# Starting a kernel's mixing projection inside the last attention pair

## The reference, cut to what matters

```python
def mla_group(...):                       # 8 heads of 64
    q = rms_norm(q, g_qnorm); k = rms_norm(k, g_knorm)      # then rope on 32 of 96 columns
    pr = softmax(mask(q @ k.T * scale)); o = pr @ v
    o = rms_norm(o, g_attn_out)           # per head
def rwkv7_group(...):                     # 8 heads of 64
    ...                                   # y: layer norm per head, * ln_x_w + ln_x_b, + bonus
    return y * g
h = h + concat([mla, rwkv]) @ w_o_2       # 1024 x 1024: the "mix" stage
h = h + peer_ffn(rms_norm(h), ...)        # the next stage
```

## Time and profile before

| | us |
|---|---|
| median of three runs | 2223.5 |
| the profiled execution | 2227.96 |
| its span in the trace | 2226.2 |
| TensorE busy, of the span | 2168.6 (97%) |
| VectorE busy | 1467.3 (66%) |
| ScalarE busy | 1021.1 (46%) |
| mean granted TensorE clock | 0.991 |

### The profile page before, as it was taken

How to read it: one execution, slowest core, us unless ns; L and a number is a source line. 1 busy time by engine, 2 the same in 40 slices (tenths; PEclk the granted TensorE clock), 3 DMA queues, 4 the chain that set the end, 5 groups by cost and what they waited for, 6 DMA issues and landing times.

```text
span 2226.2 us, 42388 instructions
## 1 busy us (share of the span) xinstructions
PE 2168.6 (97%) x15414; PEld 1945.2 (87%) x15428; DVE 1467.3 (66%) x2785; ACT 1021.1 (46%) x1734; POOL 59.3 (3%) x59
## 2 busy tenths in 40 slices
PE   9999999999999999999998889999999999999999
PEld 7999998899899977999987558889888999999998
DVE  5556997655655556655765556989886666666665
ACT  4345775434534346443641343338634444444443
POOL 0000000000010000000000000110000000000000
PEclk9999999999999999999999989999999999999999
DMA  6555654455476534555511023434576666665664
GB/s 216 190 179 180 214 175 147 158 187 182 164 235 193 198 107 140 177 180 189 180 58 32 19 94 128 144 129 158 182 248 215 225 207 206 206 183 188 187 185 136
DMA packets 107727, 374.14 MB, mean 168 GB/s; under 512 B 11985, under 2 KB 17889, under 8 KB 107377
## 3 DMA queue, kind: packets, MB, share of 16 engines
q1 hardware_dynamic: 102848, 354.88, 48.6%
q0 software_dynamic: 4784, 18.00, 2.8%
HBM read 362.29 MB, written 13.69 MB: 169 GB/s over the span
## 4 chain that ended last, share of the span: by engine, by line
PE 92%; DVE 5%; ACT 1%; DVEq 1%; issue 1%; DMA 0%; ACTq 0%; POOL 0%
PE bank L351 70%; PE bank L380 8%; PE bank L1613 3%; PE bank L2513 3%; DVE w_lo L303 1%; PE bank L600 1%; PE bank L333 0%; ACT w_hi L298 0%; PE bank L618 0%; PE bank L335 0%; PE bank L2129 0%; PE bank L340 0%; DVE arena L1985 0%; PE bank L2465 0%; PE bank L2153 0%
## 5 line engine op out<-in xcount | busy, mean ns | idle before, releaser
L303 DVE TENSOR_TENSOR w_lo<-ring,w_hi 128x1024 fp32r<-128x1024 f32 x576 | 696.7, 1223 | 407.8 <-ACT w_hi L298 405.5
L298 ACT ACTIVATE w_hi<-ring 128x1024 fp32r<-128x1024 f32 x581 | 605.8, 1057 | 617.3 <-PE bank L351 561.5
L351 PE MATMUL bank<-u_hi,w_hi 128*128 128x256 f32 x2568 | 728.5, 284 | 1.9 <-DVE w_lo L303 1.9
L351 PE MATMUL bank<-u_hi,w_lo 128*128 128x256 f32 x2568 | 726.7, 283 | 0.0
L351 PE MATMUL bank<-u_lo,w_hi 128*128 128x256 f32 x2568 | 726.6, 283 | 0.0
L351 PEld LDWEIGHTS bank<-u_hi,w_hi 128*128 128x128 f32 x2568 | 492.2, 192 | 12.5 <-DVE w_lo L303 4.0
L351 PEld LDWEIGHTS bank<-u_lo,w_hi 128*128 128x128 f32 x2568 | 492.2, 192 | 7.4 <-issue 0.5
L351 PEld LDWEIGHTS bank<-u_hi,w_lo 128*128 128x128 f32 x2568 | 492.2, 192 | 0.0
L351 PE MATMUL bank<-w_hi,x_hi 128*128 128x512 f32 x992 | 391.5, 395 | 2.7 <-DVE x_lo L2719 1.3
L351 PE MATMUL bank<-w_lo,x_hi 128*128 128x512 f32 x992 | 389.3, 392 | 0.0
L351 PE MATMUL bank<-w_hi,x_lo 128*128 128x512 f32 x992 | 386.8, 390 | 0.0
(11 more groups left out here) (312 smaller groups left out, 1782.5 us busy)
## 6 DMA issues: line engine op xcount, KB each, us to landing
ring<-in_w SPq DMA_DIRECT2D x264, 512.0 KB, 3.7
ring<-in_expert_u SPq DMA_DIRECT2D x128, 512.0 KB, 3.5
ring<-in_expert_v SPq DMA_DIRECT2D x128, 512.0 KB, 4.2
ring<-in_ssm_in SPq DMA_DIRECT2D x40, 512.0 KB, 4.5
gate_dram<-con SPq DMA_DIRECT2D x16, 576.0 KB, 2.8
arena<-gate_dram POOLq DMA_DIRECT2D x9, 1024.0 KB, 8.6
ring<-in_ssm_out SPq DMA_DIRECT2D x16, 512.0 KB, 4.1
ring<-in_w_o SPq DMA_DIRECT2D x16, 512.0 KB, 3.6
```

Of the source, the lines that this page charges most:

```text
L298: act.activation(w_hi[slot][:, :], ring[slot][:, :], ACT.Copy).then_inc(hi_made[slot], 1)
L303: dve.tensor_tensor(w_lo[slot][:, :], ring[slot][:, :], w_hi[slot][:, :].bitcast(F32), ALU.subtract).then_inc(freed[slot], 1)
L351: mm = pe.matmul(out, left[a], right[b], start=start and n == 0, stop=stop and n == 2, skip_group_check=True)
```

## The change

Three things are altered; nothing that is computed changes.

- The mix stage's eight closings are taken in the order of tiles 4, 5, 6, 7, 0, 1, 2, 3 (recurrent tiles first), in slots 2, 3, 0, 1, 2, 3, 0, 1, and written out without loops. TensorE clears the accumulators and runs closings 0 and 1 between the scores and the probabilities of pair 3, closing 2 between probabilities and outputs, closing 3 between the outputs and `output_squares(3)`. Closings 4 to 7 follow behind it. The last two keep their order by quarters. ScalarE's and VectorE's splits for closings 0 to 5 are placed in the mla stage by hand.
- SyncE loads the first two weight tiles between the second and the third load of the mla heads, the other six behind the fourth.
- The seven passes on `y_rw` go into two of VectorE's waits for the rotation: L2299, L2302 and L2313 into `turn_head(1, 0)`, L2315 into `turn_head(2, 0)`.

```diff
+        MIX_OUT = ((2, 0), (3, 0), (0, 0), (1, 0), (2, 1), (3, 1), (0, 1), (1, 1))
+        MIX_TILE = (4, 5, 6, 7, 0, 1, 2, 3)
+        def mix_close(pe, p, quarters=range(4)):
+            n, i = MIX_OUT[p]
+            pe.wait_ge(S("left_ready"), left_no("mix_out", 0, p) + 1)
+            close_split(pe, p % 2, n, "mix_out", i, p == 7, quarters)
+        def mix_left_hi(act, p):
+            if p > 1:
+                m, j = MIX_OUT[p - 2]
+                split_done(act, m, "mix_out", j)
+            if p < 4:
+                act.wait_ge(S("m_max"), 5)
+            else:
+                act.wait_ge(S("mo_ready"), MIX_TILE[p] + 1)
+            act.activation(x_hi[:, p % 2, :], mix_all[:, MIX_TILE[p], :], ACT.Copy).then_inc(S("left_hi"), 1)
@@ mla_sync
             for i in range(4):
                 load(sp, i % 2, io["mla_u"][i, :, :], "mla_heads", i // 2)
+                if i == 1:
+                    mix_load(sp, 0)
+                    mix_load(sp, 1)
+            for p in range(2, 8):
+                mix_load(sp, p)
@@ mla_tensor
                     head_keys(pe, i + 1, 1)
+                else:
+                    pe.wait_ge(S("mo_ready"), 3)
+                    clear_acc(pe, upd["mix"])
+                    mix_close(pe, 0)
+                    mix_close(pe, 1)
                 turn_probs(i)
                 if more:
                     head_squares(pe, i + 1, 1)
                     turn_halves(i + 1, 0)
+                else:
+                    mix_close(pe, 2)
                 outputs(i)
+            mix_close(pe, 3)
             output_squares(3)
@@ mla_scalar
                     square_head(act, i + 1, 1)
+                else:
+                    mix_hi(act, 3)
+                    mix_left_hi(act, 2)
+                    mix_left_hi(act, 3)
                 for a in range(2):
                     act.wait_ge(S("mp_turned"), 2 * i + a + 1)
...
                     root_head(act, i + 1, 1)
+                else:
+                    mix_hi(act, 4)
+                    mix_left_hi(act, 4)
                 act.wait_ge(S("mo_done"), i + 1)
                 act.activation(mo_sq, group(i)[3][:, 0:T], ACT.Square).then_inc(S("mo_squared"), 1)
+                if i < 2:
+                    mix_hi(act, i)
+                elif i == 2:
+                    mix_left_hi(act, 0)
+                    mix_left_hi(act, 1)
+                else:
+                    mix_hi(act, 5)
+                    mix_left_hi(act, 5)
                 act.wait_ge(S("mo_summed"), i + 1)
                 rstd(act, mo_root, group(i)[2][:, 0:T], HD, stat[:, 14:15]).then_inc(S("mo_rooted"), 1)
+                if i == 2:
+                    mix_hi(act, 2)
@@ mla_vector, turn_head: between L2288 and L2290
+                if (i, a) == (1, 0):
+                    scale_recurrent()
+                if (i, a) == (2, 0):
+                    gate_recurrent()
+                if (i, a) == (3, 0):
+                    mix_lo(dve, 0)
@@ mla_vector, the loop
             for i in range(4):
                 for a in range(2):
+                    if i == 3:
+                        if a == 1:
+                            mix_lo(dve, 1)
+                        mix_left_lo(dve, a)
                     dve.wait_ge(S("m_scores"), 2 * i + a + 1)
...
                         turn_head(i + 1, a)
+                else:
+                    for p in range(2, 6):
+                        mix_lo(dve, p)
+                        mix_left_lo(dve, p)
                 dve.wait_ge(S("mo_rooted"), i + 1)
@@ the mix stage
         def mix_tensor(pe):
-            pe.wait_ge(S("mo_ready"), 4)
-            out_tensor(pe, "mix_out", upd["mix"])
+            mix_close(pe, 4)
+            mix_close(pe, 5)
+            for quarters in (range(3), (3,)):
+                mix_close(pe, 6, quarters)
+                mix_close(pe, 7, quarters)
```

More of the change, by code:

```diff
@@ L397, in clear_acc @@
                           skip_group_check=True)
[L402 to L405, removed]
         def left_no(stage, i, n):
@@ L410, in left_no @@
             return sum(4 * RING_PLAN[r][0] for r in order[:order.index(stage)]) + 4 * i + n
[L412 to L450, removed]
         ATTN_OUT = ((2, 0), (3, 0), (0, 0), (1, 0), (2, 1), (0, 1), (1, 1), (3, 1))
@@ L2111, in mla_sync, with mix_load, mix_hi, mix_lo @@
                 load(sp, i % 2, io["mla_u"][i, :, :], "mla_heads", i // 2)
+                if i == 1:
[5 more added lines that the diff above has]
+        MIX_TILE = (4, 5, 6, 7, 0, 1, 2, 3)
+        def mix_load(sp, p):
+            n, i = MIX_OUT[p]
+            load(sp, n, io["w_o2"][MIX_TILE[p], :, :], "mix_out", i)
+        def mix_close(pe, p, quarters=range(4)):
+            n, i = MIX_OUT[p]
+            pe.wait_ge(S("left_ready"), left_no("mix_out", 0, p) + 1)
+            close_split(pe, p % 2, n, "mix_out", i, p == 7, quarters)
+        def mix_hi(act, p):
+            n, i = MIX_OUT[p]
+            make_hi(act, n, "mix_out", i)
+        def mix_left_hi(act, p):
[7 more added lines that the diff above has]
+            act.activation(x_hi[:, p % 2, :], mix_all[:, MIX_TILE[p], :], ACT.Copy).then_inc(S("left_hi"), 1)
+        def mix_lo(dve, p):
+            n, i = MIX_OUT[p]
+            make_lo(dve, n, "mix_out", i)
+        def mix_left_lo(dve, p):
+            dve.wait_ge(S("left_hi"), left_no("mix_out", 0, p) + 1)
+            dve.tensor_tensor(x_lo[:, p % 2, :], mix_all[:, MIX_TILE[p], :], x_hi[:, p % 2, :].bitcast(F32),
+                              ALU.subtract).then_inc(S("left_ready"), 1)
         def head_banks(i):
@@ L2292, in turn_head, with scale_recurrent, gate_recurrent @@
                 dve.tensor_tensor(qk_rope[Q_, a, :], qk_cos[Q_, a, :], qk_sin[Q_, a, :], ALU.add).then_inc(S("mqk_ready"), 1)
+            def scale_recurrent():
+                dve.wait_ge(S("y_rw_rooted"), 1)
+                dve.tensor_tensor(y_rw, y_rw, rw_tmp, ALU.mult)
+                dve.drain()
+                for p in range(4):
+                    dve.tensor_scalar(y_rw[:, p, :], y_rw[:, p, :], V("lnw", p, p + 1), V("lnb", p, p + 1), ALU.mult, ALU.add)
+                dve.drain()
+                dve.tensor_tensor(y_rw, y_rw, bonus, ALU.add)
+            def gate_recurrent():
+                dve.tensor_tensor(y_rw, y_rw, g_gate, ALU.mult)
             for a in range(2):
@@ L2311, in mla_vector @@
                     dve.tensor_scalar(m_stat[:, a, 1, :], m_stat[:, a, 0, :], -1.0, None, ALU.mult).then_inc(S("m_max"), 1)
[L2312 to L2315, removed]
                 for a in range(2):
@@ L2331, in program @@
         SYNC["mla"], TENSOR["mla"], SCALAR["mla"], VECTOR["mla"] = mla_sync, mla_tensor, mla_scalar, mla_vector
-        def mix_sync(sp):
-            out_sync(sp, "mix_out", io["w_o2"])
         def mix_tensor(pe):
-            pe.wait_ge(S("mo_ready"), 4)
-            out_tensor(pe, "mix_out", upd["mix"])
+            mix_close(pe, 4)
[3 more added lines that the diff above has]
+                mix_close(pe, 7, quarters)
         def mix_scalar(act):
-            act.wait_ge(S("mo_ready"), 4)
-            out_scalar(act, "mix_out", mix_all)
+            for p in (6, 7):
+                mix_hi(act, p)
+                mix_left_hi(act, p)
+            lead_next_hi(act, "mix")
         def mix_vector(dve):
-            out_vector(dve, "mix_out", mix_all)
-        SYNC["mix"], TENSOR["mix"], SCALAR["mix"], VECTOR["mix"] = mix_sync, mix_tensor, mix_scalar, mix_vector
+            for p in (6, 7):
+                mix_lo(dve, p)
+                mix_left_lo(dve, p)
+            lead_next(dve, "mix")
+            update_h(dve, 1.0, upd["mix"], "mix_out", last_slot=MIX_OUT[7][0])
+        TENSOR["mix"], SCALAR["mix"], VECTOR["mix"] = mix_tensor, mix_scalar, mix_vector
         TG, SETS, SCALED = 4, 4, 2
```

## The result

The changed kernel takes 2213.36 us (median of five runs, 2209.33 to 2216.62) against 2224.85 us of the kernel before in the same runs: a ratio of 0.9948, interval 0.9937 to 0.9959. That is 11.5 us, or 0.5%. The forecast had the direction and most of the size, but it said 2208.5 and at most 2213.0, so the time lies just outside its range.

A forecast was written before the change was run, and what follows sets the result against it. TensorE, 92% of the chain, was taken as the bound, losing time where idle or slowly clocked. 12.0 + 3.0 = 15.0 us off 2227.96 gave 2213.0, less 4.5 to the median 2208.5; range 2206.0 to 2213.0.

The forecast's parts named there:

- Part 1: Closings moved into the last pair: last scores to last closing takes 25.7 us in place of 37.7, gaining 12.0 us.
- the hand-over before closing 2: Last pair: VectorE's splits for closing 2 come slightly late, so TensorE stands up to 0.3 us.
- the delay of the probabilities: Last pair: VectorE's splits delay the probabilities by 1.8 us, covered by clearing and closings 0 and 1 with 0.5 spare.
- ScalarE's order: Last pair: splits for closings 2 and 3 precede the copies of the probabilities; copies done at 1314.3, outputs follow at once.
- the weights: Weight loads: cost 0, the tightest having about a microsecond to spare; if one is late, up to 1 us.
- Part 2: Recurrent passes moved out of pair 0: 1.49 us idle goes, pair 1's second rotation starts earlier, 3.0 us gained.
- no fall: Pair 1: the clock stays at 1.00 behind the new gap of about 1.8 us; forecast chance 0.55.
- rival A: Clock falls in pair 1's new gap, before the closings or in the peer stage, taking back 1.5 to 3.4 us; 0.33.
- The carry-over of 4.5 us: The median of the runs lies 4.5 us below the profiled execution; carried over, 2213.0 becomes 2208.5.
- B: Last pair: a wait of 3 us or more replaces the idle time; 2219 to 2221 us, about no change; 0.06.
- C: Hand-overs between closings and short work keep the clock at 0.50: last pair 10.8 us slower, 2231.3 us; 0.02.

The follow-up runs named there:

- e6: Changed kernel with closing 1 taken behind the probabilities of pair 3 instead of ahead of them: 2216.58 us, ratio 0.9960.
- e5: Kernel before with TensorE's waits in pairs 0 and 3 and behind pair 3's output squares filled by matmuls on zeros: 2219.43 us, ratio 0.9976.
- e8: Kernel before, unchanged, run once more for a second profile: 2224.24 us.
- e10: Kernel before with six matmuls on zeros in the 2.1 us gap at the start of the peer stage: 2224.29 us, ratio 0.9995.
- e1: Changed kernel with the seven recurrent passes put back where they were, so only the closings moved: 2214.27 us, ratio 0.9951.
- e2: Kernel before with only the seven recurrent passes moved, closings left where they were: 2224.50 us, ratio 0.9998.
- e11: Changed kernel, unchanged, run again for a second profile: 2215.01 us.
- e12: Changed kernel, unchanged, run a third time for another profile: 2209.85 us.
- e13: Changed kernel, unchanged, timed again: 2211.20 us, ratio 0.9946.
- e4: Changed kernel with seven matmuls on zeros in TensorE's gap before the second rotation of pair 1: 2210.21 us, ratio 0.9938.
- e9: Kernel before, closings unmoved, recurrent passes spread: times the root before pair 0's second scores, the rest in pair 1's wait: 2221.93 us, ratio 0.9985.
- e14: Changed kernel with the first recurrent pass (times the root) moved into VectorE's wait before pair 0's second scores: 2210.41 us, ratio 0.9938.
- e7: Changed kernel, first recurrent pass moved into VectorE's wait before pair 0's second scores, six zero matmuls before the peer stage's first queries: 2210.78 us, ratio 0.9932.

## Why the prediction was right or wrong

**Part 1, 12.0 us: right.** The last pair takes 25.83 us where 25.7 were forecast; the hand-over before closing 2 is 0.43 where 0.3 were, the delay of the probabilities was 1.8 and covered (by 0.3 us; e6 shows that it is needed), ScalarE's order did no harm, the weights were there. Against the five traces with the closings in the old place and nothing filled there (36.99 to 38.30) it is 11.2 to 12.5 us. 3.1 to 4.4 of them are clock (e5). The time of the whole kernel agrees less closely: the three stretches of the first pair of traces differ by 37.70 - 25.83, 50.87 - 51.19 and 882.43 - 880.32, together 13.7 us, the two medians by 11.5. All 12 runs of the changed kernel give 2212.7, which is 11.8 to 13.2 under the medians of the kernel before beside the experiments; the median of the first five happens to lie 0.7 us above that.

**Part 2, 3.0 us: wrong, and this step failed.** Idle times and starts came out as forecast: no wait before the probabilities of pair 0, a gap of 1.75 us, the second rotation 3.0 us earlier relative to the first scores (1270.37 less 1254.26 is 16.11; before, 1274.32 less 1255.20 is 19.12). But the 3.0 compares a before whose clock had fallen with an after whose clock had not. Like with like it is 47.79 to 47.94 without a fall and 50.87 to 51.19 with one: a loss of 0.15 to 0.3 us. The move took away 1.5 us of idle time and put 1.75 in its place. The prediction wrote "This needs a clock of 1.00 throughout, where before 7 us ran at 0.52" and still booked the whole as a gain of the passes. Of four traces with the old gap of 1.49 us open (before, e8, e10, e1) three have the fall, of six with the new one four: moving the gap changed its place and hardly its risk. e2's ratio of 0.9998 is the plain measurement.

**The gap and the clock.** The forecast took "no fall", rival A the fall at 0.33. With this gap open six traces exist (changed, e2, e6, e11, e12, e13), and in four of them the clock fell. A's price, 1.5 to 3.4 us, was right (3.25 by e4), its chance too low; "the gap is nearest in size to the 1.83 that left the clock alone" was no ground, since one and the same 1.74 us gap did both in e11 and e12. So did the 1.83 us gap itself. In e2, with the same instructions, TensorE's timeline and the windows have a fall behind it:

```profile
1159.05 3.11 PE L1613 MATMUL bank<-arena 64*64 64x64 f32 x64 [1.83 <-DVE arena L1967]
```
```profile
1160.00:1164.00 4.00, 4.00 (x48) 3.62 (x45) 1.12 (x5) 1.08 (x2) 0.00 (x0) 0.60 0.02 4
```

**The carry-over of 4.5 us.** The profiled execution of before took 2227.96 us, and the prediction subtracted 15.0 and then the distance to the median. That execution had its clock low more than e8 (0.991 against 0.994). Its span is 3.8 us longer than that of e8, and by the table 3.08 of them are the fall in pair 0, 0.48 the last pair, 0.24 the rest. So the fall in pair 0 that made up part 2's 3.0 is also most of what sets that execution above e8. To book it as the change's gain and then to carry over the whole distance counts it twice against an execution without it; the median execution itself wasn't traced. The base was low too: 2223.5 was the median of three runs, five gave 2224.85. From 2208.5 to 2213.36 it is 4.9 us: 1.35 from the base, 3.5 from a gain of 11.5 in place of 15.0. Taken between the two profiled executions, the change gave 2227.96 - 2213.36 = 14.6 us, and its terms by the table are 11.87 (last pair) - 0.32 (pairs) + 2.11 (behind) + 0.94 (upstream, not the change's). The sum of 15.0 looks right there only because the last two terms, which it didn't have, stand in for part 2.

**What it didn't have.** The 1.9 us behind the last closing. With closings in the old place and that gap open the clock fell in four traces of four (before, e8, e2, e9); with moved closings in one of nine (e14). In the other kernel with old closings and a held clock, e5, it didn't fall. Why a gap of 1.6 to 2.2 us is followed by a fall in one case and seldom in the other, when TensorE had run at full clock for some 20 us and more ahead of it in both, stays open; it wasn't tried apart.

**The rivals B and C** didn't happen. No hand-over of the changed kernel kept TensorE waiting for more than 0.43 us, and the clock stayed at 1.00 for all 96 closing matmuls between their short companions. The Trainium skill (page "TensorE: Matmul & The Clock Gate", section "A second HAM failure mode: psum-queue depth-cycling") tells of a kernel whose clock swung between its levels as it cycled through PSUM banks with short idle moments. That didn't show here: cycling through four banks with hand-overs of up to 0.46 us, 1.22 in e6, didn't move the clock from the clearing to the last closing in any of the ten traces with closings in the new place.

## What to carry to other kernels

Work that waits for nothing in the last step of a pipeline is worth most in front of the waits that have no next step to hide them: here 8 us of idle time and 3 to 4 us of clock came back. Passes that are moved into an engine's pause have to fit into it at its new length; 3.8 us in a pause of under 2 only moved the stall, and taking 1.2 us of them elsewhere made them pay. And when a profile shows a fall of the clock in the place that a change is to mend, compare with a second trace of the same kernel before its cost is booked as the change's gain.

## What the runs showed of the hardware

A single idle gap of TensorE of 1.5 to 2.1 us was followed by a fall of the granted clock to 0.50 in some executions and not in others, with the same instructions around it: 3.1 us for the one in pair 0 (before against e8; 1.3 in e10), 3.25 for the one in pair 1 (e11 against e12: 3.24). The size of the gap alone doesn't decide it. Two gaps upstream are open in all 16 traces: behind the one of 1.83 us the clock fell in one trace (e2), behind the one of 1.99 us, 26 us later, in 13 (not in e4, e5 and e12). Matmuls on zeros, about 0.24 us each, kept the clock at 1.00 in every gap that they filled (e4, e5, e7, e10), and where TensorE waits anyway they cost nothing that the traces show: in e4 the second rotation starts 16.11 us after the first scores, as in the changed kernel, and e5 gained 5.3 to 6.4 us with 27 of them and no wait removed. The scatter of this kernel goes with the clock too. The changed kernel's five first runs order themselves by their mean clock, 2209.33 us at 0.999, 2212.08 and 2213.36 at 0.997, 2214.39 at 0.996 and 2216.62 at 0.995.
